# Layer 0 of a two-layer MoE backbone: the down weights of expert 3 loaded outside the weight slots, into dead temporaries of the routing

## What is computed

```python
def grouped_moe(h, router_w, router_bias, w_gate, w_up, w_down):
    scores = jax.nn.sigmoid((h @ router_w).astype(jnp.float32))
    ...                       # best group of 4 experts, top 2 in it, weights gates (T, 16)
    out = jnp.zeros_like(h)
    for e in range(N_EXPERTS):
        y = (jax.nn.silu(h @ w_gate[e]) * (h @ w_up[e])) @ w_down[e]
        out = out + gates[:, e:e + 1].astype(h.dtype) * y
    return out

for l in range(DEPTH):
    ...                       # modulation, mixer l, gated residual
    f = grouped_moe(tokens, router_w, router_bias, exp_w_gate[l], exp_w_up[l], exp_w_down[l])
    x = x + g2 * f            # layer 0: context and latent tokens; layer 1: latent tokens alone
return rmsnorm(x_l, final_norm_g)
```

## Time and profile before

| what | us |
|---|---|
| median of three timed runs | 945.4 |
| lowest and highest of them | 944.49, 949.64 |
| the profiled execution | 949.39 |
| its span | 947.4 |
| TensorE busy (86% of the span) | 811.4 |
| DVE, ACT, POOL busy | 450.4, 268.7, 195.1 |
| data moved by DMA | 309.44 MB, mean 327 GB/s |
| expert stage of layer 0, first product to last | 281 to 525 |
| expert stage of layer 1, first product to last | 716 to 939 |

### The profile page before, as it was taken

One profiled execution on the slowest core, in us unless ns is written; L12 is line 12 of the kernel. 1 busy time (PEld: TensorE's weight loads), 2 busy tenths in 40 slices (PEclk: granted clock), 3 DMA queues, 4 the chain that ended last, 5 costly groups with the idle time before them and its releaser, 6 DMA issues. The chain is left out here.

```text
span 947.4 us, 31607 instructions
## 1 busy us (share of the span) xinstructions
PE 811.4 (86%) x13370; PEld 541.3 (57%) x13370; DVE 450.4 (48%) x1104; ACT 268.7 (28%) x474; POOL 195.1 (21%) x364
## 2 busy tenths in 40 slices
PE   2799999999969899989789599999967885586886
PEld 2444444444457777777677445467445764465674
DVE  2379999953564344444334453765262320122223
ACT  2313535431413222322222221255132220121222
POOL 2200000010044344444333500000004220111221
PEclk9999999999979999999999799999998996888998
DMA  9995399376385999999999998973658999999991
GB/s 346 348 387 194 116 376 330 122 288 258 143 338 201 401 407 409 413 408 408 408 401 395 327 386 314 396 301 138 253 200 324 407 402 424 421 405 417 423 384 46
DMA packets 70718, 309.44 MB, mean 327 GB/s; under 512 B 9752, under 2 KB 10192, under 8 KB 54256
## 3 DMA queue, kind: packets, MB, share of 16 engines
q1 hardware_dynamic: 54608, 275.78, 73.9%
q0 software_dynamic: 15040, 30.22, 9.0%
q10 hardware_dynamic: 992, 2.26, 0.6%
HBM read 297.38 MB, written 14.20 MB: 329 GB/s over the span
## 5 line engine op out<-in xcount | busy, mean ns | idle before, releaser
L801 PE MATMUL ps<-weight_ring,arena 128*32 128x128 f32 x5760 | 178.1, 284 | 34.9 <-DMA weight_ring<-in_exp_w_up 28.4
L801 PEld LDWEIGHTS ps<-weight_ring,arena 128*32 128x32 f32 x5760 | 168.8, 115 | 49.8 <-issue 41.8
L1776 ACT ACTIVATE arena<-ps 128x64 f32<-128x64 f32 x128 | 28.6, 223 | 352.7 <-PE ps L801 351.2
L1381 DVE TENSOR_TENSOR arena<-arena,ps 128x64 f32<-128x64 f32 x128 | 28.3, 221 | 210.5 <-ACT arena L1776 210.5
L588 PE MATMUL ps<-hT,weight_ring 128*128 128x512 f32 x256 | 114.7, 603 | 2.6 <-DMA weight_ring<-in_ev_w_in 2.3
L811 PE MATMUL ps<-weight_ring,arena 128*32 128x256 f32 x1440 | 92.9, 382 | 5.0 <-issue 2.9
L1089 DVE SCALAR_TENSOR_TENSOR arena<-arena,par 128x512 f32<-128x512 f32 x132 | 94.9, 750 | 4.0 <-DVE arena L1120 0.8
L801 PE MATMUL ps<-arena 128*32 128x128 f32 x2432 | 76.7, 287 | 19.4 <-DMA arena<-in_exp_w_up 17.5
L801 PEld LDWEIGHTS ps<-arena 128*32 128x32 f32 x2432 | 72.8, 116 | 25.5 <-issue 24.5
L588 PEld LDWEIGHTS ps<-hT,weight_ring 128*128 128x128 f32 x256 | 48.1, 192 | 67.2 <-issue 63.3
L1776 ACT ACT_TABLE_LOAD x64 | 82.1, 1283 | 6.6 <-DVEq L1346 1.5
(11 more groups left out here) (321 smaller groups left out, 895.7 us busy)
## 6 DMA issues: line engine op xcount, KB each, us to landing
weight_ring<-in_ada_w SPq DMA_DIRECT2D x24, 2048.0 KB, 14.4
weight_ring<-in_exp_w_up SPq DMA_DIRECT2D x22, 2048.0 KB, 10.6
weight_ring<-in_exp_w_down SPq DMA_DIRECT2D x22, 2048.0 KB, 10.6
weight_ring<-in_exp_w_gate SPq DMA_DIRECT2D x22, 2048.0 KB, 10.5
arena<-in_exp_w_up SPq DMA_DIRECT2D x10, 2048.0 KB, 11.0
arena<-in_exp_w_gate SPq DMA_DIRECT2D x10, 2048.0 KB, 10.9
hT<-in_exp_w_down SPq DMA_DIRECT2D x10, 2048.0 KB
weight_ring<-in_ev_w_in SPq DMA_DIRECT2D x4, 2048.0 KB, 13.1
```

The source lines that it names most:

```text
L801: last = mm(ps[32 * qd:32 * qd + 32, 1 + hh, 0:P].rearrange("p (m n) -> p m n", m=2), xgT[:, MT * k:MT * k + MT], w2[:, k, :, at:at + 64], ...
L1381: v.tensor_tensor(act_in[:, half], act_sl[:, half], ps[:, 1 + hh, 64:P], ALU.mult).then_inc(s_ac[l], 1)
L1776: s.activation(act_sl[:, 64 * hh:64 * hh + 64], ps[:, 1 + hh, 0:64], ACT.Silu).then_inc(s_sl[l], 1)
```

## The change

In layer 0 the down matrix of expert 3 is not loaded into slot 2. It goes, in three pieces, into `arena` columns 13088 to 15136, `arena` columns 3072 to 4096, and `after_lru`. `HELD` names the experts treated so: expert 3 in layer 0, none in layer 1. Slot 2 then takes the down matrix of expert 6 at the place in SP's order where that of expert 3 stood. `g2_mat` moves to `ada_part`, and so does the tile result of layer 1 (`y_1`). The loads of `qg`, `kg` and `trig` move from the front of POOL's tile loop to behind the result gathers of layer 0. SP's loop over experts is written out, one expert after another, in both layers; the rule "two places earlier has landed" stays, kept in the list `earlier`.

```diff
+HELD = ((3,), ())
...
-    moe_n = [TRIOS + (i in (0, 2)) for i in range(3 * SETS)]
+    moe_n = [TRIOS + (i in (0, 2)) - (i in [3 * (e % SETS) + 2 for e in HELD[0]]) for i in range(3 * SETS)]
...
-        g2_diff, g2_lat, g2_mat = reg(12576, 256), reg(12832, 256), reg(13600, 256)
+        g2_diff, g2_lat, g2_mat = reg(12576, 256), reg(12832, 256), ada_part[:, 256:512]
...
+        y_1 = ada_part[:, 0:256]
...
+        held_parts = [{3: ((0, 2048, reg(13088, 2048)), (2048, 1024, reg(3072, 1024)), (3072, 1024, after_lru))},
...
+        def down_columns(l, e, step, c0, c1):
+            if e not in HELD[l]:
+                return deep(3 * (e % SETS) + 2)[:, step, c0:c1]
+            for at, n, memory in held_parts[l][e]:
+                if at <= D * step < at + n:
+                    return memory[:, D * step - at + c0:D * step - at + c1]
...
+            def load_held(l, e, i):
+                at, n, memory = held_parts[l][e][i]
+                rows = a["exp_w_down"][l][e].rearrange("(h p c) n -> p h (c n)", h=2, p=P)
+                sp.dma_start(memory, rows[:, at // 2048, at % 2048:at % 2048 + n]).then_inc(landed[SPARE], 16)
+
+            def load_behind(l, e, m, end, earlier):
+                expert_done(l, end, m)
+                sp.sem_inc(s_par, 1)
+                sp.wait_ge(*earlier[-2])
+                load(l, e, e % SETS, m)
+                earlier.append((landed[3 * (e % SETS) + m], landed_count(l, e, m)))
...
-                with sp.Fori(1, TRIOS) as trio:
-                    for b in range(SETS):
-                        end = sp.value_load(ctl[0:1, bass.ds(trio * SETS + (b - SETS), 1)], min_val=1, max_val=MAXTILES)
-                        load_expert(l, trio * SETS + b, b, lambda m: expert_done(l, end, m), trio)
-                end = sp.value_load(ctl[0:1, E - 1 - SETS:E - SETS], min_val=1, max_val=MAXTILES)
-                load_last(l, end)
+                earlier = [(landed[7], landed_count(l, 2, 1)), (landed[8], landed_count(l, 2, 2))]
+                if l == 0 and HELD[0]:
+                    sp.wait_ge(s_mst, 64)
+                    for i in range(3):
+                        load_held(0, 3, i)
+                    earlier.append((landed[SPARE], spare_count[0]))
...
+                for e in range(SETS, E):
+                    end = sp.value_load(ctl[0:1, e - SETS:e - SETS + 1], min_val=1, max_val=MAXTILES)
+                    load_behind(l, e, 0, end, earlier)
+                    if e < E - 1:
+                        load_behind(l, e, 1, end, earlier)
+                    if e - SETS not in HELD[l]:
+                        load_behind(l, e + SETS if e in HELD[l] else e, 2, end, earlier)
...
-                        if final and m == 1:
-                            pe.wait_ge(landed[SPARE], 16 * (l + 1))
+                        if e == E - 1 and m == 1 or e in HELD[l] and m == 2:
+                            pe.wait_ge(landed[SPARE], spare_count[l])
                             return
...
-                if not l:
-                    pool.wait_ge(s_id, 2)
-                    g.dma_start(qg, a["at_q_norm_g"].to_broadcast([P, DH])).then_inc(s_rope, 16)
-                    g.dma_start(kg, a["at_k_norm_g"].to_broadcast([P, DH])).then_inc(s_rope, 16)
-                    g.dma_start(after_lru[:, 3 * SEQ:4 * SEQ].rearrange("p (t n) -> p t n", t=2),
-                                a["rope"].rearrange("(t p) n -> p t n", p=P)).then_inc(s_rope, 16)
...
             rounds = moe(0)
+            g.dma_start(qg, a["at_q_norm_g"].to_broadcast([P, DH])).then_inc(s_rope, 16)
+            g.dma_start(kg, a["at_k_norm_g"].to_broadcast([P, DH])).then_inc(s_rope, 16)
+            g.dma_start(after_lru[:, 3 * SEQ:4 * SEQ].rearrange("p (t n) -> p t n", t=2),
+                        a["rope"].rearrange("(t p) n -> p t n", p=P)).then_inc(s_rope, 16)
```

More of the change, by code:

```diff
@@ L312, in deep, with landed_count @@
             return slot_memory(slot).rearrange("p (k n) -> p k n", k=4)
+        held_parts = [{3: ((0, 2048, reg(13088, 2048)), (2048, 1024, reg(3072, 1024)), (3072, 1024, after_lru))},
+                      {3: ((0, 2048, x[:, 0:CT, :].rearrange("p t d -> p (t d)")),
+                           (2048, 2048, x[:, CT:NT, :].rearrange("p t d -> p (t d)"))),
+                       4: ((0, 2048, reg(2048, 2048)), (2048, 2048, reg(13600, 2048)))}]
+        spare_count = [16 * (1 + sum(len(held_parts[0][e]) for e in HELD[0]))]
+        spare_count.append(spare_count[0] + 16 * (1 + sum(len(held_parts[1][e]) for e in HELD[1])))
+        def down_columns(l, e, step, c0, c1):
[4 more added lines that the diff above has]
+                    return memory[:, D * step - at + c0:D * step - at + c1]
+        def landed_count(l, e, m):
+            slot = 3 * (e % SETS) + m
+            passed = sum(h < e and h % SETS == e % SETS for h in HELD[l]) if m == 2 else 0
+            return 16 * (ahead[l][slot] + e // SETS + 1 - passed)
         def last_gate_and_up():
@@ L448, in experts @@
                 sp.wait_ge(s_id, 2 + 2 * l)
[L449 to L454 removed]
+                earlier = [(landed[7], landed_count(l, 2, 1)), (landed[8], landed_count(l, 2, 2))]
[4 more added lines that the diff above has]
+                    earlier.append((landed[SPARE], spare_count[0]))
+                if l and HELD[1]:
+                    if 3 in HELD[1]:
+                        sp.wait_ge(s_pos, 3)
+                        load_held(1, 3, 1)
+                    if 4 in HELD[1]:
+                        load_held(1, 4, 0)
+                        sp.wait_ge(s_mst, 128)
+                        load_held(1, 4, 1)
+                    earlier.append((landed[SPARE], spare_count[1]))
+                for e in range(SETS, E):
[5 more added lines that the diff above has]
+                        load_behind(l, e + SETS if e in HELD[l] else e, 2, end, earlier)
             experts(0)
@@ L772, in combine_tile @@
                         rows = slice(32 * qd, 32 * qd + 32)
-                        last = mm(ps[:, 4 + qd, 256 * t:256 * t + 256], spread[rows, P * t:P * t + P], y_sb[0][rows, :],
+                        last = mm(ps[:, 4 + qd, 256 * t:256 * t + 256], spread[rows, P * t:P * t + P], y_1[rows, :],
                                   start=False, stop=False, skip_group_check=True)
@@ L782, in moe, with tiles_of @@
                 down_bank = (4, 3)[l]
-                def tiles_of(trio, b, first, end):
-                    final = isinstance(trio, int) and trio == TRIOS
-                    w2, wd = last_gate_and_up() if final else gate_and_up(b), deep(3 * b + 2)
+                def tiles_of(e, first, end):
+                    w2 = last_gate_and_up() if e == E - 1 else gate_and_up(e % SETS)
                     def weights(m):
-                        if final and m == 1:
-                            pe.wait_ge(landed[SPARE], 16 * (l + 1))
+                        if e == E - 1 and m == 1 or e in HELD[l] and m == 2:
+                            pe.wait_ge(landed[SPARE], spare_count[l])
                             return
-                        pe.wait_ge(landed[3 * b + m], 16 * trio + 16 * (ahead[l][3 * b + m] + 1))
+                        pe.wait_ge(landed[3 * (e % SETS) + m], landed_count(l, e, m))
                     with pe.Fori(first, end) as g:
@@ L832, in moe @@
                         first, end = end, tile_end(e)
-                    tiles_of(e // SETS, e % SETS, first, end)
+                    tiles_of(e, first, end)
                 if l:
@@ L1399, in moe @@
                         dve.wait_ge(s_dn[l], g + 1)
[L1400 removed]
+                        v.tensor_tensor(y_1, ps[:, 3, 0:256], g2_mat, ALU.mult).then_inc(s_y[l], 1)
                     else:
```

3 lines of the change are left out of this document (1 added, 2 removed).

## The result

The changed kernel takes 942.09 us (median of ten runs, 938.22 to 944.75), the kernel before 948.46 us (ten runs, 944.49 to 949.78). The ratio is 0.9935, with a 95% interval of 0.9912 to 0.9959: 6.2 us faster (3.9 to 8.3 by the interval). Forecast were 939.7 us and a gain of 5.65, which lies well inside the interval. The absolute time is 2.4 us off: the three runs of before that were known (median 945.4) lay 3.1 us under the median of ten, and the gain came out larger by some 0.7 us.

The account below looks back on a forecast made before the run. Layer 0's expert stage was taken as near balance, with the weight stream on the DMA engines limiting it late. One load spacing, 5.65 us, all other terms zero, off 945.4 gave 939.7 us, range 936.7 to 944.0.

Parts of the forecast that it names:

- The mechanism: Layer 0, 281 to 296 us: expert 3's down matrix loads while DMA engines are mostly idle, shortening the later weight stream.
- The early load is free: End of layer 0's routing: load issued at 280.8 us, landed near 289, before expert 3's gate load; no cost.
- Rival 1: Layer 0's first tiles: early load delays gathers and the stream behind them by 2 us; gain 3.65, 941.8 us; chance 0.08.
- My sign for it: Layer 0: expert 3's gate load going out later than 296.5 us would show the early load delaying the first tiles.
- Worth of a load: Layer 0's weight stream: removing one 2 MB load saves one spacing, 5.65 us, range 5.2 to 5.8.
- TensorE with the shorter stream: Layer 0, experts 11 to 13: some waits vanish, 2.5 us at D12, about 3 at U13; all 5.65 us arrives.
- The small loads: Layer boundary: moving gain vectors and rotary table, 256 KB, costs zero, range 0 to 1.9 us, hidden behind TensorE's DVE wait.
- Rival 2: Layer boundary: 1.9 us of the gain lost to the 256 KB or an unmoved wait; 941.7 us; chance 0.13.
- Straight code on SP: SP's expert loop written out in both layers: zero cost, since two loads are in flight.
- Rival 4: Layer 1's 37 loads: SP's straight code makes them late; 0.3 us per load gives 950.9 us; chance 0.05.
- Its sign: Layer 1: load spacings above 5.2 us would show that SP's straight code slows the stream.
- The high end of the range: Whole kernel: 944.0 us, said to take in early-load delay, layer-boundary loss and 2 us for TensorE hold-ups.

Follow-up runs that it names:

- the second: The changed kernel timed again, unaltered, beside the kernel before, with a second profile: 943.2 us, ratio 0.9956 (0.9931 to 0.9981).
- the second profile of before: The kernel before, unaltered, timed as a subject of its own against itself and profiled again: 948.1 us, ratio 1.0000.
- extra sets: Changed kernel with two more copies of the gain vectors and rotary table loaded at the layer boundary, 768 KB instead of 256 KB: 947.0 us, ratio 0.9991 to the kernel before.

## Why the prediction was right

- **The mechanism**: right. D3 alone in the hole makes the gain, shown by taking each half away: the change without the held load, and the held load issued in the stream instead of in the hole, both give the time of before.
- **The size**: partly luck. The 6.2 us of the first measurement are above the forecast and the 4.2 of the second below it; a gain of this size is known to some 2.3 us from one comparison. The first passes the 0.5% that the prediction had set, the second (0.44%) does not. The firm number is the trace's 5.1.
- **The early load is free**: right. It goes out at 280.37 (280.8 forecast), is over by about 289, and leaving it out changes neither G3 in the first pattern nor the stretch behind it; the times alone would allow a price of a microsecond or so. Rival 1 with its 2 us is out. My sign for it, G3 later than 296.5, was a bad one: G3 was at 296.71, and the kernel without an early load has that too.
- **Worth of a load**: 5.65 us was taken; 5.4 was measured at U13 and 5.1 at D14 and the stage's end, just outside the bounds of 5.2 to 5.8. The prediction took U13 for the last wait and missed D14. The 5.23 at U13 was the nearer of its two rows, but not because the end hangs there: at D14 the spacing of landings is 6.6 us (499.63 to 506.27). The bytes at the mean rate of the stream, 2.097 MB at 402 GB/s, give 5.2 us, which comes as near; that it is the rate that sets the worth is my reading. By the 358 GB/s of the Trainium skill (DMA: Bandwidth & Descriptors, section "Bandwidth") the worth would be 5.9 us, an estimate that is further off; the stretch from 296 to 526 again moved 401 GB/s. The same section has 425 GB/s for a 16 MB transfer by a core alone and gives some 358 GB/s to each core when both of a pair stream, and this kernel runs on one core.
- **TensorE with the shorter stream**: right in its order. No wait for D11 and U12, expert 12's first products at 3.70 us. The 2.5 us of waiting for D12 came out at 0.52 in this profile: TensorE was ready at 466.6 instead of 465.1 and D12 in at 467.1 instead of 467.7. The delay of TensorE fits the slow first tile and a slow batch around 428 us, which took of the reserve as it was meant to; in the second profile, without the slow first tile, the wait is 2.41. U13 is waited for 3.24 us (3 forecast).
- **The small loads**: zero is not contradicted, but the reason was wrong. I hid them behind 1.98 us of waiting for DVE, from one execution; the second profile of before has 0.35 us there, and a wait of 2.84 for the load itself. The room was not a constant of the kernel. The price of a set, 0.7 us by bytes, is too low: extra sets cost 1.7 to 1.9 us each in time. Rival 2 with its 1.9 us for the one set is not seen in any time, and a part of a microsecond of it stays possible.
- **Straight code on SP**: zero, as forecast; 5.19 us per load in layer 1, and 0.9997 for the code without the held load. Rival 4 is out. Its sign, spacings above 5.2, was too fine: profiles with the straight code have 5.18 to 5.26, the two profiles with the loop 5.20 and 5.21.
- **The absolute time**: 2.4 us too low, from the median of three runs of before. The high end of the range, 944.0, is 0.2 more than its working gives for one rival with the 2 us (941.8 + 2), and both rivals at once would have needed 945.7; the measured 942.1 lies inside by any of these.

## What to carry to other kernels

Look for a hole on the DMA engines right ahead of a stream that never idles, and for memory that is dead just then: a load that fits in the hole was worth 5.1 us here, near the 5.2 us that its bytes take at the rate of the stream, and nothing when it kept its place in the stream. Single spacings between landings, 5.2 to 6.6 us, are a poorer guide, and the last load that the consumer waits for can be one with a wait of under 1 us. Before costing such a change, see what the stream hangs on, and measure stages from that event: from G3's issue the gain showed to some 0.6 us in single profiles, while whole executions scatter by several. A wait or a gap seen in one profile is not yet room; two profiles of the same kernel had 1.98 and 0.35 us of it.

## What was not expected of the hardware

Fast filler products were followed by a slower stage. Where the fillers of the routing ran in 1.97 us instead of 3.7, TensorE idled 1.67 us, and the first expert tile then ran with the granted clock at 0.50 to 0.62 over its first 3 us and took about 5 us instead of 3.70, in eight of eight such executions, while with 3.7 us of fillers and no idle time it kept the full clock in five of five. With the idle time cut to 0.80 us the clock stayed up in the one execution seen. Whether the idle time is the cause, or the low clock only falls now on the fillers (0.50 there in the five) and now on the tile, is not shown. The kernel's run-to-run scatter of several us has at least this source: G3 at 295.5 to 295.9 in the one case, 296.7 to 298.9 in the other.
